# Hybrid decoder step on one Trainium2 core: feed-forward weight units taken two by two, passes alternating between PSUM banks

## The reference, cut to what matters

```python
x = x + jnp.sum(gates * proj, axis=-2) @ w_o
h = rmsnorm(x, norm_ffn) @ w_up                 # 1024 -> 4096
x = x + jnp.square(jax.nn.relu(h)) @ w_down     # 4096 -> 1024
```

## Time and profile before

| what | value |
|---|---|
| median of 3 runs | 949.95 us |
| the profiled execution | 949.91 us |
| its span in the trace | 948.1 us |
| PE (matmul) busy | 943.3 us, 99% |
| PEld (weight load) busy | 914.9 us, 96% |
| DVE (VectorE) busy | 669.3 us, 71% |
| ACT (ScalarE) busy | 483.8 us, 51% |
| POOL (GpSimd) busy | 43.2 us, 5% |
| DMA moved | 164.25 MB |

### The profile page before, as it was taken

The page is one execution under the profiler, slowest core; times in us unless marked ns, Lnnn a source line. Parts: engine busy times, 40 slices in busy tenths (PEclk is TensorE's granted clock), DMA queues, the critical chain, the costliest instruction groups (busy, mean ns, idle before and its releaser), DMA issues.

```text
span 948.1 us, 18976 instructions
## 1 busy us (share of the span) xinstructions
PE 943.3 (99%) x7944; PEld 914.9 (96%) x7944; DVE 669.3 (71%) x1052; ACT 483.8 (51%) x707; POOL 43.2 (5%) x61
## 2 busy tenths in 40 slices
PE   9999999999999999999999999999999999999998
PEld 8999898999999999999999998989999999999998
DVE  6798798858876755555757887889498676556463
ACT  6429663473664353535553586436537644435351
POOL 0070000000000000000001500000000000000000
PEclk9999999999999999999999999999999999999999
DMA  9655444444554585455475563534444546555542
GB/s 361 219 186 172 184 145 134 135 134 152 156 182 153 192 300 176 156 172 161 162 253 164 189 219 113 166 123 147 135 145 156 182 147 244 172 163 172 160 155 91
DMA packets 44276, 164.25 MB, mean 173 GB/s; under 512 B 4992, under 2 KB 6528, under 8 KB 43648
## 3 DMA queue, kind: packets, MB, share of 16 engines
q1 hardware_dynamic: 42912, 152.95, 49.1%
q0 software_dynamic: 1136, 9.83, 2.7%
q10 hardware_dynamic: 144, 0.26, 0.1%
HBM read 153.29 MB, written 10.29 MB: 173 GB/s over the span
## 4 chain that ended last, share of the span: by engine, by line
PE 97%; DMA 1%; ACT 0%; SPq 0%; DVE 0%; issue 0%; DVEq 0%; ACTq 0%
PE pz L413 90%; PE pm L413 6%; DMA raw<-in_w 1%; PE pm L579 1%; ACT w_hi L783 0%; DVE arena L1022 0%; PE pm L632 0%; PE pm L642 0%; SPq L356 0%; SPq L350 0%; PE pm L531 0%; SPq L360 0%; DVE arena L1054 0%; DVE xp L1058 0%; ACT rstd L801 0%
## 5 line engine op out<-in xcount | busy, mean ns | idle before, releaser
L413 PE MATMUL pz<-a_hi,w_hi 128*128 128x288 f32 x1376 | 413.2, 300 | 0.9 <-DVE a_lo L1027 0.6
L413 PE MATMUL pz<-a_lo,w_hi 128*128 128x288 f32 x1376 | 405.9, 295 | 0.0
L413 PE MATMUL pz<-a_hi,w_lo 128*128 128x288 f32 x1376 | 404.8, 294 | 0.0
L783 ACT ACTIVATE w_hi<-raw 128x1024 fp32r<-128x1024 f32 x266 | 278.0, 1052 | 208.5 <-PE pz L413 196.7
L1013 DVE TENSOR_TENSOR w_lo<-raw,w_hi 128x1024 fp32r<-128x1024 f32 x266 | 327.4, 1231 | 10.8 <-ACT w_hi L783 10.8
L413 PEld LDWEIGHTS pz<-a_hi,w_hi 128*128 128x128 f32 x1376 | 257.9, 187 | 10.5 <-issue 8.6
L413 PEld LDWEIGHTS pz<-a_hi,w_lo 128*128 128x128 f32 x1376 | 259.0, 188 | 0.0
L413 PEld LDWEIGHTS pz<-a_lo,w_hi 128*128 128x128 f32 x1376 | 258.3, 188 | 0.3
L413 PE MATMUL pz<-h_hi,w_hi 128*128 128x288 f32 x768 | 228.2, 297 | 0.0
L413 PE MATMUL pz<-h_lo,w_hi 128*128 128x288 f32 x768 | 226.5, 295 | 0.0
L413 PE MATMUL pz<-h_hi,w_lo 128*128 128x288 f32 x768 | 225.8, 294 | 0.0
(11 more groups left out here) (175 smaller groups left out, 539.9 us busy)
## 6 DMA issues: line engine op xcount, KB each, us to landing
raw<-in_w SPq DMA_DIRECT2D x267, 512.0 KB, 3.5
arena<-in_s SPq DMA_DIRECT2D x2, 2048.0 KB, 9.6
out_ss_out<-arena POOLq DMA_DIRECT2D x2, 2048.0 KB, 8.1
out_u_out<-arena POOLq DMA_DIRECT2D x2, 864.0 KB, 6.8
arena<-arena SPq DMA_DIRECT2D x8, 180.0 KB, 3.2
arena<-in_kcT SPq DMA_DIRECT2D x2, 512.0 KB, 6.9
arena<-in_vc SPq DMA_DIRECT2D x2, 512.0 KB, 7.6
out_kc_out<-in_kc_kept POOLq DMA_DIRECT2D x1, 992.0 KB, 7.0
```

What stands on the lines that cost most here:

```text
L413: return nc.tensor.matmul(out, a, b, start=start, stop=stop, **kw)
L783: act_fn(w_hi[:, r], raw[:, r], ACT.Copy).then_inc(s["w_hi"], 1)
```

## The change

`ffn_turn` now steps through the units two by two. A new helper `pair` goes over k once for both units, and each of the three passes is done for the first unit and then for the second, into the two tiles' banks. Both `unit_done` signals come on the last two matmuls. `norm_sum` and `new_state` stand after the pair instead of after the unit. In the last turn of a layer units 12 to 15 stay single. VectorE does the split of unit j + 3 ahead of the wait for unit j where j is even and belongs to a pair; where j is odd or single it stays after the read. ScalarE and SyncE are unchanged.

```diff
@@ -68,6 +68,7 @@
 UNITS = U_FFN + FI * 16
 RING = 4
 LEAD = 3
+SINGLE = 12
 UW = 1024
 X_PIECES = ((0, 1), (1, 4), (4, 6), (6, 8))
 
@@ -426,6 +427,22 @@
                     if n == 0 and first_done is not None:
                         last.then_inc(first_done, 1)
                 last.then_inc(s["unit_done"], 1)
+
+            def pair(outs, g, rhs_hi, rhs_lo, have=None):
+
+                hi, lo = ([w[:, (g + n) % RING].rearrange("p (k c) -> p k c", k=KT) for n in range(2)]
+                          for w in (w_hi, w_lo))
+                for k in range(KT):
+                    if have is not None:
+                        have(k)
+                    for n in range(2):
+                        mm(outs[n], hi[n][:, k], rhs_hi(k), start=k == 0, stop=False)
+                    for n in range(2):
+                        mm(outs[n], hi[n][:, k], rhs_lo(k), start=False, stop=False)
+                    for n in range(2):
+                        last = mm(outs[n], lo[n][:, k], rhs_hi(k), start=False, stop=k == KT - 1)
+                        if k == KT - 1:
+                            last.then_inc(s["unit_done"], 1)
 
             def unit(l, u):
 
@@ -730,22 +747,31 @@
                     rows = slice(h * NS, (h + 1) * NS)
                     mm(PM[h], ktok_s[rows], imask[rows, q:q + 4].rearrange("p b n -> p (b n)")).then_inc(s["snew"], 1)
 
-            def ffn_turn(l, i, first=False):
-                for j in range(16):
+            def ffn_turn(l, i, first, last):
+                for j in range(0, 16, 2):
                     u = U_FFN + j
-                    pe.wait_ge(s["w_lo"], l * UNITS + i * 16 + (u + 1) + HEAD)
-                    pe.wait_ge(s["z_read_dve"], i * 16 + read_dve(l, T_FFN + j - 4))
-                    out = [PZ[bank(l, T_FFN + j)][:, 0:T]]
+                    single = last and j >= SINGLE
                     if j < 8:
-                        have = (lambda k: pe.wait_ge(s["a_lo"], l * 16 + (9 + k))) if first and j == 0 else None
-                        product(out, l * UNITS + u, lambda k: a_hi[:, k], lambda k: a_lo[:, k], KT, have)
+                        rhs_hi, rhs_lo = (lambda k: a_hi[:, k]), (lambda k: a_lo[:, k])
                     else:
-                        have = (lambda k: pe.wait_ge(s["f_lo"], l * 8 * FI + i * 8 + (k + 1) + HEAD)) if j == 8 else None
-                        product(out, l * UNITS + u, lambda k: h_hi[:, k], lambda k: h_lo[:, k], KT, have)
+                        rhs_hi, rhs_lo = (lambda k: h_hi[:, k]), (lambda k: h_lo[:, k])
+                    have = None
+                    if first and j == 0:
+                        have = lambda k: pe.wait_ge(s["a_lo"], l * 16 + (9 + k))
+                    if j == 8:
+                        have = lambda k: pe.wait_ge(s["f_lo"], l * 8 * FI + i * 8 + (k + 1) + HEAD)
+                    outs = [PZ[bank(l, T_FFN + j + n)][:, 0:T] for n in range(2)]
+                    for n in ((0, 1) if single else (1,)):
+                        pe.wait_ge(s["w_lo"], l * UNITS + i * 16 + (u + n + 1) + HEAD)
+                        pe.wait_ge(s["z_read_dve"], i * 16 + read_dve(l, T_FFN + j + n - 4))
+                        if single:
+                            product(outs[n:n + 1], l * UNITS + u + n, rhs_hi, rhs_lo, KT)
+                        else:
+                            pair(outs, l * UNITS + u, rhs_hi, rhs_lo, have)
                     if first and j == 0:
                         norm_sum(2 * l + 2)
-                    if first and j in (7, 12):
-                        new_state(l, 0 if j == 7 else 4)
+                    if first and j in (6, 12):
+                        new_state(l, 0 if j == 6 else 4)
 
             for name in ("unit_done", "nsum", "pool_y"):
                 pe.sem_inc(s[name], HEAD)
@@ -761,7 +787,7 @@
                     pooling(l, u)
                     hgrn(l, u)
                 for i in range(FI):
-                    ffn_turn(l, i, first=i == 0)
+                    ffn_turn(l, i, i == 0, i == FI - 1)
 
 
         @block.scalar
@@ -1335,6 +1361,10 @@
 
             def mlp(l, i, last, first=False):
                 for j in range(16):
+                    g = l * UNITS + U_FFN + i * 16 + j + LEAD
+                    early = j % 2 == 0 and not (last and j >= SINGLE)
+                    if early and g < DEPTH * UNITS:
+                        split(g)
                     if j < 8:
                         dve.wait_ge(s["unit_done"], l * UNITS + i * 16 + (U_FFN + j + 1) + HEAD)
                         if first and j == 0:
@@ -1350,8 +1380,7 @@
                         if first:
                             for q in {8: (0,), 9: (1,), 10: (2,), 11: (3,), 13: (4,), 14: (5,), 15: (6, 7)}.get(j, ()):
                                 new_state(l, q)
-                    g = l * UNITS + U_FFN + i * 16 + j + LEAD
-                    if g < DEPTH * UNITS:
+                    if not early and g < DEPTH * UNITS:
                         split(g)
                     if last and j >= 8 and l + 1 < DEPTH:
                         input_lo(2 * l + 3, j - 8, lambda k: pr(l, "norm_next", k))
```

## The result

The changed kernel takes 961.49 us, the median of five runs (959.66 to 962.71), against 949.90 before (949.72 to 950.46). The ratio is 1.0118, 95% interval 1.0107 to 1.013. The profiled execution took 961.62 us, 11.7 more than the 949.91 of before.

The account below looks back on a forecast made before the run. It took TensorE's number of matmuls times the distance between their starts as the bound. 949.91 + 2.6 (first wait) + 7.2 (second) + 2.2 (clock) + 0 (distance) = 961.9, given as 962.0 us; range 958 to 968.

Parts of the forecast that it names:

- No gain from alternating: Matmuls inside pairs: switching banks at each matmul leaves their distance at 0.133 us, so 0 gain.
- the 38 us at the upper end: Largest gain considered for alternating banks: 0.013 us off each of 2880 paired matmuls.
- First wait: Feed-forward entry, unit 70: TensorE waits for `w_lo` of unit 71, 1.31 us lost, once per layer.
- Second wait: Feed-forward entry, after norm_sum: rounding of unit 73 stands behind `norm`, so TensorE loses 3.61 us, once per layer.
- Clock: TensorE's idle time of about 3.3 us at norm_sum lets the granted clock fall: 1.1 us per layer, 2.2 for both.
- the 2.2 at the upper end: Largest clock loss considered per layer: 4.4 us at half rate, as bounded by the kernel's start.
- the middle: Clock loss taken between the ends 0 and 2.2 per layer: 1.1 us.
- Chains of later splits: Later pairs: their splits come in time, room 0.7 us, 0.15 at j = 6; 0 taken, at most 1.6 us.

## Why the prediction was right, point by point

**No gain from alternating.** Right in kind. The step over a unit's end already showed that a matmul into another bank comes no sooner. The pairs are 0.027 us shorter, 1.6 of the 38 us at the upper end, and the kernel with a third of the bank changes has the same. The estimate of 122.5 ns, worked out from what the Trainium skill (TensorE: Matmul & The Clock Gate, Back-to-back issue gap) gives for an isolated matmul, was not reached by any order of passes tried: 132.8 ns was the least mean over a pair with 288 columns.

**First wait.** 1.31 forecast, 1.22 measured: the restart costs 0.16 (0.05 after the split's end, and 0.10 for the late second matmul) and not the 0.22 taken from the kernel's start.

**Second wait.** The steps off today's rows held to 0.02 us: Ln + 0.82, rounding + 1.70, split + 2.77, its end + 3.99. TensorE went on at 280.39, 0.06 after the split's end, where 0.15 had been taken, and the late second matmul added 0.10. 3.99 + 0.16 - 0.62 = 3.53, in place of 3.61. The run with the rounding moved shows that the order in ScalarE's queue is the cause.

**Clock.** The fall itself was right, the size was off: 1.52 per fall in place of 1.1. Two steps behind the 2.2 at the upper end were too dear: the slow stretch was 3.41 us long where the kernel's start gave 4.4, and it costs 0.44 of its length and not half, since matmuls come 0.240 us apart in it and not 0.27. The reason given for the middle, that a part of the stretch could lie in the idle time, did not hold in the changed kernel's profile: the fall came 1.09 and 0.74 us behind the end of the gap, and all of it was paid. It did hold in other runs: in layer 1 of the kernel with the banks changing at every third matmul the fall came 0.48 us before the end (1.31 us lost), with the units in turn 0.90 and 0.58 us before it, and in layer 0 of the former the clock did not fall at all. So no single number was to be had; 1.1 lies inside what the runs do, below their middle.

**Chains of later splits.** Right: by the unit ends of layer 0 the second turn's pair (2, 3), for which a bound of 0.2 had been given because of the state operations, was late by 0.03 us, and the pairs behind j = 6 not at all, though the room worked out was only 0.15. The chain to j = 8, for `h_lo`, was not worked out; it holds in the changed kernel by the slower use of the blocks, which the kernel with the units in turn showed by losing 1.2 us there.

**What lay outside the terms.** 0.7 us in layer 1's attention. The sum hit 961.5 within half a us since the errors offset: 0.3 too much for the waits, 0.8 too little for the clock, and 1.6 gained by the pairs and 0.8 lost (0.7 in that attention, 0.1 in later pairs) that it did not have. The mechanism was right; that the total came so close is luck.

**Readings that were off.** There are three, and the sum does not use the first two. ScalarE's Ln comes 8.41 us after the last matmul of unit 69 where it came 4.02 before, so 4.4 later and not 6.4 + 1.2: what moves it is the end of the pair (7.6) in place of the end of unit 70 (3.2). TensorE's idle time in the second wait ran from +0.78 (the end of norm_sum) to +4.05 and not from +0.9 to +4.15. And the slow matmuls were 0.24 apart and not 0.27.

## What to carry to other kernels

When a signal is moved behind a longer piece of work (here norm_sum behind a pair), look in every queue for what stands behind the operation that waits for it, and ask whether the next piece of work needs one of those: here a rounding that was ready to go stood behind a norm, and the producer waited for its own consumer's queue. Pairing units halves the number of points at which buffers come free, so each pair needs two inputs ready ahead instead of one; interleaving them pays by slowing the use of each input block, not by the banks. An idle gap of TensorE is to be priced with the slow clock that can follow it: here up to 1.5 us per stretch on top of a gap of 3.3, and with it a spread of the times, since the clock does not fall at every such gap.

## What the runs showed of the hardware that I had not expected

After an idle gap of 3.27 us the granted clock fell 1.09 and 0.74 us behind the return of the matmuls (changed kernel), 0.48 us before it (layer 1 of the kernel with the banks changing at every third matmul), or not at all (layer 0 of the same kernel), and stayed at the lower level for 3.41 us, once for 6.83 (layer 0 of the kernel with the units in turn). It fell as well in the kernel without early splits, whose matmuls come in stretches of 6.4 us with waits of 1.8 us on average between them, a mean of 0.967 over that kernel. A few idle matmuls in the gap kept it up and took the spread of the times away.

A matmul of 128x128 weights in fp32r comes every 133.3 ns with 288 columns and every 118.9 ns with 256, about a ninth above the column time, whatever bank it goes to. At the lower clock it comes every 240 ns with 288 columns, which is the column time alone.
